# Attention of a two-layer encoder: probabilities scaled on GpSimd and transposed plainly, instead of products with diagonals

## The reference

```python
def windowed_gqa(h, w_qkv, sink, w_o, rel_bias):
    nb = seq // SWA_BLOCK                      # 4 blocks of 128 queries
    # 16 query heads of 64, 4 key/value heads; each block sees 3 blocks of keys
    kb, vb = band(k), band(v)
    s = jnp.einsum('bnqkgd,bnskd->bnkgqs', q, kb) * (SWA_HEAD_DIM ** -0.5)
    s = jnp.where(mask, s + bias, NEG_INF)
    p = jax.nn.softmax(jnp.concatenate([s, sink_col], axis=-1), axis=-1)[..., :-1]
    o = jnp.einsum('bnkgqs,bnskd->bnqkgd', p, vb).reshape(bsz, seq, qd)
    return o @ w_o
```

## Time and profile before

| | us |
|---|---|
| median of 3 runs | 1761.19 (1756.18 to 1762.73) |
| the profiled execution, its own time | 1760.08 |
| its span in the profile | 1758.0 |
| TensorE (PE) busy | 1412.1 (80%) |
| VectorE (DVE) busy | 543.7 (31%) |
| ScalarE (ACT) busy | 247.2 (14%) |
| GpSimd (POOL) busy | 172.9 (10%) |

### The profile page before, as it was taken

How to read it: one execution, slowest core, us unless ns; L and a number is a source line. 1 busy time by engine, 2 the same in 40 slices (tenths; PEclk the granted TensorE clock), 3 DMA queues, 4 the chain that set the end, 5 groups by cost and what they waited for, 6 DMA issues and landing times. The chain is left out here.

```text
span 1758.0 us, 18695 instructions
## 1 busy us (share of the span) xinstructions
PE 1412.1 (80%) x7013; PEld 686.5 (39%) x7013; DVE 543.7 (31%) x1125; ACT 247.2 (14%) x501; POOL 172.9 (10%) x215
## 2 busy tenths in 40 slices
PE   6999756995988878878875989894997878878872
PEld 3444745552333333323322457653333323323330
DVE  6998589124111111101114038424111101101104
ACT  2201222110100000000002027411100000000001
POOL 0007070001100000000002000001100000000002
PEclk9999877996999999989997989996999989989996
DMA  7510502426999999999996200406899999999994
GB/s 236 150 66 15 49 13 97 203 101 264 392 403 413 404 410 413 410 404 410 407 395 231 80 17 1 192 36 255 348 392 411 409 407 410 408 403 412 405 418 168
DMA packets 75027, 486.05 MB, mean 276 GB/s; under 512 B 16752, under 2 KB 23536, under 8 KB 50016
## 3 DMA queue, kind: packets, MB, share of 16 engines
q1 hardware_dynamic: 53984, 440.26, 63.5%
q0 software_dynamic: 9472, 23.94, 4.3%
q10 hardware_dynamic: 11520, 21.15, 3.2%
HBM read 465.91 MB, written 27.79 MB: 281 GB/s over the span
## 5 line engine op out<-in xcount | busy, mean ns | idle before, releaser
L588 PE MATMUL psum<-ring,work 128*64 128x512 f32 x992 | 494.9, 657 | 128.4 <-DMA ring<-in_moe_w_up 125.7
L589 PE MATMUL psum<-ring,work 128*64 128x512 f32 x992 | 495.9, 658 | 0.0
L588 PEld LDWEIGHTS psum<-ring,work 128*64 128x64 f32 x992 | 145.1, 151 | 449.8 <-issue 446.2
L601 PE MATMUL psum<-ring,work 128*64 128x512 f32 x992 | 226.5, 598 | 31.1 <-DVE work L739 31.1
L736 DVE TENSOR_TENSOR work<-work,psum 64x512 f32<-64x512 f32 x64 | 44.2, 690 | 639.4 <-ACT work L693 566.4
L693 ACT ACTIVATE work<-psum 64x512 f32<-64x512 f32 x64 | 37.8, 590 | 839.9 <-PE psum L589 839.9
L589 PEld LDWEIGHTS psum<-ring,work 128*64 128x64 f32 x992 | 145.0, 151 | 0.0
L601 PEld LDWEIGHTS psum<-ring,work 128*64 128x64 f32 x992 | 66.6, 136 | 145.0 <-issue 125.1
L742 DVE COPY work<-psum 128x512 f32<-128x512 f32 x64 | 44.2, 691 | 247.7 <-PE psum L601 247.7
L1527 PE MATMUL psum<-ring,hT 128*128 128x512 f32 x256 | 112.1, 600 | 2.1 <-ACT work L1646 2.1
L883 POOL COPY ints<-ints 64x1 uint32 (+1 forms) x64 | 11.4, 178 | 816.6 <-PE psum L580 772.8
(11 more groups left out here) (350 smaller groups left out, 1422.2 us busy)
## 6 DMA issues: line engine op xcount, KB each, us to landing
ring<-in_moe_w_gate SPq DMA_DIRECT2D x62, 2048.0 KB
ring<-in_moe_w_up SPq DMA_DIRECT2D x62, 2048.0 KB, 23.1
ring<-in_moe_w_down SPq DMA_DIRECT2D x62, 2048.0 KB, 23.6
y_dram<-work ACTq DMA_DIRECT2D x128, 128.0 KB
ring<-in_hyb_w_in SPq DMA_DIRECT2D x5, 2048.0 KB, 9.8
ring<-in_swa_w_qkv SPq DMA_DIRECT2D x3, 2048.0 KB, 14.3
y_dram<-ones POOLq DMA_DIRECT2D x1, 4096.0 KB, 19.9
ring<-in_hyb_w_out SPq DMA_DIRECT2D x2, 2048.0 KB, 7.7
```

Of the source, the lines that this page charges most:

```text
L588: nc.tensor.matmul(bank[2 + b][0:BLK, :], XT[b][:, c, :], g[:, c, :], start=c == 0, stop=c == KC - 1)
L589: i = nc.tensor.matmul(bank[2 + b][BLK:P, :], XT[b][:, c, :], u[:, c, :], start=c == 0, stop=c == KC - 1)
L601: i = nc.tensor.matmul(bank[6 + b][BLK * hf:BLK * (hf + 1), :], HTE[b][:, c, :], d[:, c, hf * HALF:(hf + 1) * HALF], start=c == 0, stop=c ...
```

## The change

VectorE's `scale` ends with the reciprocal, which now raises `s_dg`. GpSimd then multiplies the item's exponentials by it in place, one instruction per head with the reciprocal as a scalar per query, and raises a new counter, `s_pn`. TensorE waits for that one and transposes the scaled probabilities with the identity as the other operand. The diagonals are gone.

```diff
--- before.py
+++ after.py
@@ -1782,13 +1782,12 @@
         AT0 = 16384
         SINK = cut(WK, 16448, 16)
         BI = cut(RG, V0, AH * BAND)
-        DG = [cut(WK, 512 * b, 512) for b in range(2)]
         a_q, a_qa, a_qd, f_mm, f_ev = (Count(n) for n in ("attn_qkv", "attn_qkv_act", "attn_qkv_dve", "bias_mm", "bias_rows"))
         sk_in = sem("sink_loaded")
         a_in, f_st, bi_ld = sem("attn_small_loaded"), sem("bias_stored"), sem("bias_loaded")
-        s_mm, s_b, s_m, s_e, s_t, s_te, s_o, s_oe, s_dg = (Count(n) for n in (
+        s_mm, s_b, s_m, s_e, s_t, s_te, s_o, s_oe, s_dg, s_pn = (Count(n) for n in (
             "scores", "scores_biased", "scores_max", "probs", "probs_transposed", "probs_evac", "attn_out",
-            "attn_out_evac", "probs_diagonals"))
+            "attn_out_evac", "probs_sums_inverted", "probs_normalized"))
 
         def keys(n):
             lo, hi = max(0, n - 1), min(NT, n + 2)
@@ -1845,14 +1844,13 @@
 
                 n, g = ITS[it]
                 lo, hi, _ = keys(n)
-                pe.wait_ge(s_dg.s, it + 1)
+                pe.wait_ge(s_pn.s, it + 1)
                 if it:
                     pe.wait_ge(s_te.s, it)
                 for kb in range(hi - lo):
                     for k in range(4):
-                        x = nc.tensor.matmul(bank[4 + kb][:, k * P:(k + 1) * P],
-                                             SBF[it % 4][:, BAND * k + kb * P:BAND * k + (kb + 1) * P],
-                                             DG[it % 2][:, k * P:(k + 1) * P], start=True, stop=True)
+                        x = nc.tensor.transpose(bank[4 + kb][:, k * P:(k + 1) * P],
+                                                SBF[it % 4][:, BAND * k + kb * P:BAND * k + (kb + 1) * P], ident)
                 x.then_inc(s_t.s, 1)
 
             def outp(it):
@@ -1980,11 +1978,8 @@
                 dve.wait_ge(s_e.s, it + 1)
                 V(tv.tensor_tensor(den, den, sk, ALU.add))
                 V.sync()
-                V(tv.reciprocal(rc, den))
+                V(tv.reciprocal(rc, den), s_dg)
                 V.sync()
-                if it >= 2:
-                    dve.wait_ge(s_t.s, it - 1)
-                V(tv.tensor_tensor(shp(DG[it % 2], 4, P), ins_dim(ident, 1, 4), ins_dim(rc, 2, P), ALU.mult), s_dg)
 
             for it in range(3):
                 soft(it)
@@ -1996,6 +1991,17 @@
                     soft(it + 3)
             V.sync()
             dve_add_out(dve, V, 1)
+
+        def pool_mixer1(pool, Q):
+            for it, (n, g) in enumerate(ITS):
+                lo, hi, _ = keys(n)
+                w = P * (hi - lo)
+                st = 16 * (it % 4) + AT0
+                pool.wait_ge(s_dg.s, it + 1)
+                for k in range(4):
+                    s = SBF[it % 4][:, BAND * k:BAND * k + w]
+                    Q(nc.gpsimd.tensor_scalar(s, s, WK[:, st + 12 + k:st + 13 + k], None, ALU.mult), s_pn if k == 3 else None)
+            Q.sync()
 
         wqkv_v = A["swa_w_qkv"][0].rearrange("(p c) n -> p c n", c=KC)
         wo_v = A["swa_w_o"][0].rearrange("(c p) n -> p c n", c=KC)
@@ -2079,6 +2085,7 @@
             pool_moe(pool, 0, Q)
             gain(3)
             router_loads(1)
+            pool_mixer1(pool, Q)
             gain(4)
             pool_moe(pool, 1, Q)
```

## The result

| kernel | median of the runs, us | lowest to highest | profiled execution, us | its span, us | granted clock |
|---|---|---|---|---|---|
| before (measured again beside it) | 1758.80 | 1756.18 to 1762.73 | 1760.08 | 1758.0 | 0.907 |
| after | 1778.45 | 1776.06 to 1781.69 | 1776.06 | 1774.2 | 0.898 |

The changed kernel is slower: 1.0107 of the time before, with a 95% interval of 1.0078 to 1.0136. The forecast was 1750.1, faster. By the medians the difference is 19.7 us, by the profiled executions 16.0; the profiled one of the changed kernel is the fastest of its four, and what makes the others up to 5.6 us longer isn't shown.

A forecast was written before the change was run, and what follows sets the result against it. Attention's middle items were taken as paced by TensorE, 5.93 us each. Gains of 8.4 and 3.4 less 0.9 make 10.9, stepped to the hundredth 11.1, so 1761.19 - 11.1 = 1750.1 us, range 1744 to 1762.

The forecast's parts named there:

- Products become transposes: TensorE's attention step: 12 products taking 2.87 us become transposes taking 1.31, 1.56 less per middle item.
- The diagonal goes from VectorE: VectorE in attention drops 16 diagonals of 0.69 us; its floor falls to 4.59 us per middle item.
- GpSimd's price: One GpSimd one-input multiplication in attention: 0.57 us for 384 columns (bounds 0.48 to 0.83), 0.45 for 256.
- The loop, 7.67 + 4T for two items: Middle attention items round TensorE, VectorE and GpSimd: 3.83 + 2T each, 4.97 us at T = 0.57, the new bound.
- T: Time of one GpSimd multiplication in attention's middle items, 384 columns, taken as 0.57 us.
- Granted clock 1.00 from item 1 on: TensorE in attention was to run at full clock, 2.4 GHz, from item 1, idling about 0.6 us a middle item.
- clock rival: Transposes in attention let TensorE's clock fall to 1.2 GHz: 8.5 us per middle item, total 1792; chance 0.03.
- Mutual blocking: GpSimd and VectorE's biased scores block each other: T 1.17, VectorE held 0.85 an item, 1771 us; chance 0.10, shared.
- slower still: GpSimd's attention multiplications dearer than the near-two-input-price rival (T 0.7 to 1.1); no size given; shares 0.10 with blocking.
- library reload: GpSimd's reload ahead of its attention multiplications, claimed hidden by the engine's idle time since 951.2.
- The saving or loss is passed on whole: From attention's output products on, work is unchanged, so a microsecond saved before 1131.18 is one saved at the end.
- the sum: Attention item by item: 0.9 us lost up to item 4, 8.4 gained in items 4 to 11, 3.4 in 12 to 15.

The follow-up runs named there:

- e3: Changed kernel without GpSimd's multiplications and the division; TensorE waits for the reciprocal only and transposes. Stage (first reciprocal's end to first output product) 67.1 us, pair of middle items 9.04.
- e6: Against e5: GpSimd's instruction cut into two of two heads, TensorE transposing the first two meanwhile. Median 1748.23 us, 0.9922 of the kernel before.
- e1: Changed kernel with one two-input GpSimd multiplication over an item's four heads instead of four one-input ones. Median 1752.13 us, 0.9943 of the kernel before.
- e8: Changed kernel with GpSimd multiplying only the first 128 columns of each head. Attention stage 77.6 us, pair of middle items 10.09; total not comparable.
- e4: Changed kernel with identity transposes into a free bank filling TensorE's gaps: 48 before item 0, then 14 or 6 behind outputs. Median 1768.07 us, 1.0035 of before.
- e7: Changed kernel with VectorE scaling in place by four one-input multiplications, GpSimd doing nothing. Median 1758.14 us, 0.9969 of the kernel before.
- e2: Changed kernel with GpSimd multiplying by a constant 0.01 instead of the reciprocal read by pointer. Attention stage 95.1 us, pair of middle items 13.95; total not comparable.
- e5: Against e1: 48 identity transposes added before item 0 as a warm start. Median 1753.23 us, 0.9948 of the kernel before.

## Why the prediction was wrong, step by step

- **Products become transposes: right.** 12 transposes have one record each and what follows them starts 1.46 later (1081.29 - 1079.83 in e3); the forecast had 1.31 for the 12 from the earlier trace rows, 0.15 too little, so an item saves 1.41 there and not 1.56.
- **The diagonal goes from VectorE: right.** Its floor was put at 4.59; in e3 its biased scores follow each other at 4.51.
- **GpSimd's price: this is the step that failed,** in the words "Hence 0.48 to 0.83 us for 384 columns" and "I take one read stream as lying near the first". The argument ran: writing alone costs 0.76 ns a column, reading two and writing 1.68, so reading one and writing lies between. The runs show 0.60 for 128 columns, 0.92 for 256, 1.24 for 384: 0.28 fixed and 2.52 ns a column, above both ends. The two-input row I had was exact: 512, 768, 1024 and 1536 columns take 1.04, 1.47, 1.89 and 2.75 (e6 and e1), which is 0.18 and 1.67 ns a column. A bound that rests on "less data, less time" isn't a bound between two different operations; the trace had no row of this one, and the upper end should have stayed open.
- **The Trainium skill** (GPSIMD Engine Reference, sections 3.1 and 4.1) led the same way: its 1.03 cycles an element made 0.52 us, its "1-input is roughly line-rate" a cheap instruction. The rows disagree with both for this operation: 2.52 ns a column, half as much again as with two inputs. And the "about 2x" for two inputs, which I called agreeing, is 1.05 / 0.69 = 1.5 in the rows.
- **The loop, 7.67 + 4T for two items: right** in the middle items, within 0.1, with every T that was tried while the clock was full: e8 10.09 (10.01), e1 10.49 (10.42), e4 12.67 (12.64).
- **Granted clock 1.00 from item 1 on: wrong here, for the middle items only because T was.** With waits of 0.84 to 1.76 before the middle items (e8, e1, e7) the clock stays full there; behind waits of 2.65 to 3.66 (e2 and the changed kernel) the transposes run at half of it, and about 6.5 us of the 14.8 come from that by the estimate under e4. In the last items it fell in e8, e7 and e5 as well, with waits of 1.3 at most, so a smaller T alone would not have made this step right everywhere. My clock rival had the right symptom for the wrong reason: it put it on the transposes. The Trainium skill (TensorE: Matmul & The Clock Gate, Part 4) does so too. The runs disagree: e3 and e4 are at 1.00 with the same transposes, and in e5, where TensorE has nothing but the 48 transposes from 1044 to 1050, the granted clock goes from 0.50 over 0.73 (1046 to 1048) to 1.00 (1048 to 1050).
- **Mutual blocking: not where the rival put it.** L1961 keeps its 1.76 beside GpSimd. Of the small steps it is mainly L1969 that is caught by it, up to 0.54 instead of 0.16, a mean of 225 ns over 15. The first eight multiplications (7.23 us from 1046.06, 0.90 each) have their full price although VectorE does nothing but two steps of four columns until 1053.84. The rival's T of 1.17 and its side were near the result, its mechanism was not; of a GpSimd "slower still", which is what came, I had only the name and a share of the 0.10. GpSimd was idle for 94.47 us before the first multiplication, which starts 0.10 behind the first reciprocal (1046.06 against 1045.96), so the library reload ahead of it cost nothing, as forecast.
- **The saving or loss is passed on whole: right** for after (14.8 + 1.2 against 16.0).
- **The rest.** With T = 1.24 the forecast's own loop would have said 12.6 a pair against 11.86, slower by some 0.4 an item in the eight middle ones. The stage by parts, up to the transposes of item 4, from there to those of item 12, and from there to its end: before 21.7 + 47.5 + 17.3, after 27.3 + 54.9 + 19.1. So the changed kernel loses 5.6, 7.4 and 1.8, where the sum had a loss of 0.9 and gains of 8.4 and 3.4. In e4, with the clock held and item 0 warm, it loses 3.8, 1.8 and 0.5: without the clock most of the loss is in the first items, where GpSimd takes 0.92 instead of the forecast 0.45. What the forecast had no term for is the clock.

## What to carry to other kernels

A price that no row shows has no upper bound just because it reads less than a row that does; time one instruction first, or give the chance of a bad price its full weight. When work moves to a slower engine between two steps of TensorE, count the wait it opens as well as the length of the loop: behind waits of 1.2 us the middle items here ran at the full clock, behind waits of 2.7 to 3.7 us at half of it. On GpSimd, write a scaling by one value per partition as one two-input multiplication with the value repeated, and cut it so that its consumer can start on the first part.

## What the runs showed that I had not expected

- GpSimd's one-input multiplication costs 2.52 ns a column, its two-input one (with the second input repeated along the columns) 1.67; 1536 columns take 4.97 us as four of the first kind and 2.75 as one of the second. The pointer to the scalar is only 0.07 of a fixed 0.28 (e2). Why the one-input form is dearer isn't shown, nor were other one-input operations tried.
- The same four instructions take VectorE 1.41 us and GpSimd 4.9.
- TensorE's clock fell in waits of 2.65 to 3.66 us between the bursts of the middle items and not in waits of about 1.2 there; filling the waits with transposes of the identity, which compute nothing, held it at 1.00 from 1050 to 1120 and gave back 8.7 us, 2.2 of them at the cold start (e4). The length of the last wait alone doesn't decide: in the changed kernel 8 transposes behind a wait of 2.13 (at 1066.77) took 1.09, in e2 8 behind 2.07 (at 1068.38) took 1.97, and in the last items of e5 it fell behind a wait of 1.10 that e1 went through at 1.00.
- 48 such transposes ahead of a cold stage take 7.13 us. In e5 they delay the first item by 1.3 and still bring item 4 0.9 sooner; the whole shows no gain, since the clock fell in the last items.
